# Two scaled chunks per output block, squares ahead of the last casts, and modulation dealt 5/5/2 over the thirds of a feed-forward stage

## The reference

```python
def modulate(x, g, shift, scale):
    return rmsnorm(x, g) * (1.0 + scale[:, None, :]) + shift[:, None, :]

def swiglu(h, w_gu, w_down):
    gu = h @ w_gu
    g, u = jnp.split(gu, 2, axis=-1)
    return (jax.nn.silu(g) * u) @ w_down

for l in range(DEPTH):                                  # DEPTH = 2
    mod = (c_act @ w_mod[l] + b_mod[l]).reshape(c.shape[0], N_MOD, D_MODEL)
    h = modulate(x, g_norm[l, 0], mod[:, 0], mod[:, 1])
    x = x + 0.5 * mod[:, 2][:, None, :] * swiglu(h, w_ffn1_gu[l], w_ffn1_down[l])
    h = modulate(x, g_norm[l, 1], mod[:, 3], mod[:, 4])
    x = x + mod[:, 5][:, None, :] * hybrid_mixer(h, ...)
    h = modulate(x, g_norm[l, 2], mod[:, 6], mod[:, 7])
    x = x + 0.5 * mod[:, 8][:, None, :] * swiglu(h, w_ffn2_gu[l], w_ffn2_down[l])
```

## Time and profile before

| | |
|---|---|
| runs (us) | 2893.82, 2894.48, 2900.41 |
| profiled execution (us) | 2897.52 |
| its span (us) | 2895.7 |
| mean granted TensorE clock | 0.978 |
| busy: PE, DVE, ACT, POOL | 96%, 47%, 37%, 39% |
| weights and modulation read | 368.23 MB, 130 GB/s |

### The profile page before, as it was taken

One profiled execution on the slowest core, in us unless ns is written; L12 is line 12 of the kernel. 1 busy time (PEld: TensorE's weight loads), 2 busy tenths in 40 slices (PEclk: granted clock), 3 DMA queues, 4 the chain that ended last, 5 costly groups with the idle time before them and its releaser, 6 DMA issues.

```text
span 2895.7 us, 34805 instructions
## 1 busy us (share of the span) xinstructions
PE 2777.8 (96%) x12952; PEld 2261.3 (78%) x12952; DVE 1360.8 (47%) x2214; ACT 1067.7 (37%) x1561; POOL 1140.2 (39%) x488
## 2 busy tenths in 40 slices
PE   6999999999999999999999999998989999999997
PEld 4888877778888788887777888887767778788886
DVE  5323257652324623237755242434654556673645
ACT  3222246442223422225543232354444453442322
POOL 2444443244444444444224444462211324344443
PEclk9999999999999999999999999998999999999998
DMA  7535442144445453443225353542200214222221
GB/s 284 204 117 188 155 151 88 58 161 176 159 145 187 169 182 138 174 168 124 73 73 189 139 207 132 204 164 81 73 30 15 73 61 151 102 102 102 97 92 44
DMA packets 70435, 378.82 MB, mean 131 GB/s; under 512 B 7904, under 2 KB 8672, under 8 KB 39808
## 3 DMA queue, kind: packets, MB, share of 16 engines
q1 hardware_dynamic: 65280, 358.56, 34.6%
q10 hardware_dynamic: 4992, 18.09, 1.7%
HBM read 368.23 MB, written 8.39 MB: 130 GB/s over the span
## 4 chain that ended last, share of the span: by engine, by line
PE 74%; DVE 12%; ACT 4%; issue 3%; DVEq 2%; ACTq 1%; DMA 1%; POOL 1%; SPq 1%; POOLq 0%
PE psum L514 20%; PE psum L516 20%; PE psum L515 20%; DVE psum L2152 2%; PE psum L977 2%; PE psum L999 1%; PE psum L533 1%; PE psum L535 1%; PE psum L534 1%; ACT w_hi L1092 1%; PE psum L664 1%; PE psum L665 1%; PE psum L987 1%; PE psum L666 1%; DVE psum L1655 1%
## 5 line engine op out<-in xcount | busy, mean ns | idle before, releaser
L437 POOL TENSOR_TENSOR w_lo<-raw,w_hi 128x1024 fp32r<-128x1024 f32 x464 | 1119.1, 2419 | 1566.4 <-ACT w_hi L1092 1556.3
L514 PE MATMUL psum<-h_hi,w_hi 128*128 128x512 f32 x1984 | 780.2, 393 | 14.4 <-DVE h_lo L1652 11.7
L1092 ACT CAST w_hi<-raw 128x1024 fp32r<-128x1024 f32 x464 | 480.9, 1047 | 810.0 <-PE psum L516 670.6
L515 PE MATMUL psum<-h_lo,w_hi 128*128 128x512 f32 x1984 | 775.5, 391 | 0.0
L516 PE MATMUL psum<-h_hi,w_lo 128*128 128x512 f32 x1984 | 775.5, 391 | 0.0
L514 PEld LDWEIGHTS psum<-h_hi,w_hi 128*128 128x128 f32 x1984 | 374.8, 189 | 101.2 <-DVE h_lo L1652 11.7
L516 PEld LDWEIGHTS psum<-h_hi,w_lo 128*128 128x128 f32 x1984 | 374.5, 189 | 79.1
L515 PEld LDWEIGHTS psum<-h_lo,w_hi 128*128 128x128 f32 x1984 | 374.9, 189 | 77.6 <-issue 0.5
L514 PE MATMUL psum<-hid_hi,w_hi 128*128 128x512 f32 x880 | 343.5, 390 | 5.9 <-DVE hid_lo L2158 5.9
L515 PE MATMUL psum<-hid_lo,w_hi 128*128 128x512 f32 x880 | 342.8, 390 | 0.0
L516 PE MATMUL psum<-hid_hi,w_lo 128*128 128x512 f32 x880 | 342.8, 390 | 0.0
(11 more groups left out here) (380 smaller groups left out, 3229.3 us busy)
## 6 DMA issues: line engine op xcount, KB each, us to landing
raw<-in_weights_dram SPq DMA_DIRECT2D x232, 1024.0 KB, 5.0
mod_raw<-in_mod_w_dram SPq DMA_DIRECT2D x192, 512.0 KB, 4.0
first_mods_a<-in_mod_w_dram SPq DMA_DIRECT2D x8, 512.0 KB, 11.2
first_mods_b<-in_mod_w_dram SPq DMA_DIRECT2D x8, 512.0 KB, 15.8
prod<-in_cond_rows_dram ACTq DMA_DIRECT2D x8, 512.0 KB, 3.4
first_mods_a<-gate_spill ACTq DMA_DIRECT2D x4, 1024.0 KB, 10.4
gate_spill<-gate_out_c ACTq DMA_DIRECT2D x5, 512.0 KB, 3.0
x<-in_xT_dram SPq DMA_DIRECT2D x1, 2048.0 KB, 8.5
```

The lines of the kernel that those rows point to most:

```text
L437: pool.tensor_tensor(w_lo[:, k % 2, cs], raw[:, k % 4, cs], w_hi[:, k % 2, cs].bitcast(F32), ALU.subtract).then_inc(lo_ready, 1)
L514: pe.matmul(out, wh, rhs_hi[:, c, :], start=(c == ks[0]), stop=False)
L515: pe.matmul(out, wh, rhs_lo[:, c, :], start=False, stop=False)
L1092: act.copy(w_hi[:, k % 2, cs], raw[:, k % 4, cs]).then_inc(hi_ready, 1)
```

## The change

It has five parts, all at the boundaries.

1. Scaled chunks: two per output block (0 and 1 after block 0, 2 and 3 after block 1, 4 and 5 after block 2), and 6 and 7 in the last block. For this DVE computes `a_col` earlier (`ahead_factors`, after the last up block of the last third, or after output block 0), and subtracts 0 and 1, 2 and 3, then 4, then 5 between the update of chunk 6 and its square (`last_quarter`).
2. In the last output block ACT squares chunk 6, scales it, squares chunk 7, scales it, and only then casts the second block's weights. Before, the casts stood ahead of the scaled chunks 5 to 7 (feed-forward) or ahead of both squares (mixers).
3. The bias sum is made in two parts, chunks 0 to 3 and 4 to 7, in two output blocks.
4. PE takes the column sums after the first half of chunk 2 (3 matmuls sooner) and spreads the norm after chunk 3 (6 matmuls sooner). `scale_first` becomes `scale_part`: the first bank after chunk 5 as before, the second after all 8 chunks. ACT's first SiLU waits for the first part, the copies of a mixer's and of the convolution's first block for both.
5. A third takes 5, 5 and 2 modulation positions instead of 4, 4 and 4.

```diff
+THIRD_MODS = (5, 5, 2)
-AHEAD_CHUNKS = ((), (0, 1), (2, 3, 4), (5, 6, 7))
+BIAS_PARTS = (range(0, 4), range(4, 8))
@@ PE, ahead @@
                         mm = pe.matmul(out, wl, xa_hi[:, c, :], start=False, stop=(c == KC - 1))
+                        if (c, t) == (2, 0):
+                            x_cols(r, n, i)
                     if c == KC // 2 - 1:
                         mm.then_inc(front_done, 1)
+                        rms_rows(r)
...
-                    if c == 2:
-                        x_cols(r, n, i)
-                    if c == 4:
-                        rms_rows(r)
@@ ACT @@
+            def last_chunks(i, n, xa_hi=h_hi):
+                for t in range(2):
+                    squares(n, 3, (t,))
+                    ahead(i, (6 + t,), xa_hi)
@@ ACT, first_taken (SiLU of the first block) @@
-                    act.wait_ge(scaled, first[0] + 1)
+                    act.wait_ge(scaled, 2 * first[0] + 1)
@@ ACT, ffn @@
-                        if j < 8 and j % 2 == 0 and mod in ROW_STARTS:
+                        if j < 2 * npos and j % 2 == 0 and mod in ROW_STARTS:
...
-                        if last and following is not None and j > count:
-                            ahead(following, AHEAD_CHUNKS[j - count])
+                            if following is not None:
+                                ahead(following, (2 * (j - count), 2 * (j - count) + 1))
@@ ACT, copies (mixer) @@
-                    act.wait_ge(scaled, first[0] + 1)
+                    act.wait_ge(scaled, 2 * first[0] + 2)
@@ ACT, mixer (the token mixer likewise) @@
                 for j in range(4):
+                    if j == 3:
+                        last_chunks(3 * l + 1, n + 1)
                     split_hi(g, k0 + MIX_IN_BLOCKS + j + 2, whole=(j < 2))
-                    squares(n + 1, j)
-                    if j:
-                        ahead(3 * l + 1, AHEAD_CHUNKS[j])
+                    if j < 3:
+                        squares(n + 1, j)
+                        ahead(3 * l + 1, (2 * j, 2 * j + 1))
@@ DVE @@
-            def prepare(q, following, early=0):
+            def ahead_factors(following):
                 i, g, k, at_shift, at_scale, gain, xa = following
-                if q == 1:
-                    factors(at_shift, at_scale, gain)
-                    dve.drain().then_inc(a_ready, 1)
-                if q == early:
-                    bias_sum(g, k, at_shift)
-                scaled_x(i, AHEAD_CHUNKS[q], xa)
+                factors(at_shift, at_scale, gain)
+                dve.drain().then_inc(a_ready, 1)
+
+            def prepare(q, following, early):
+                i, g, k, at_shift, at_scale, gain, xa = following
+                if early <= q < early + 2:
+                    bias_sum(g, k, at_shift, BIAS_PARTS[q - early])
+                scaled_x(i, (0, 1) if q == 0 else (2, 3) if q == 1 else (4,), xa)
+
+            def last_quarter(g, k, n, at, following):
+                i, xa = following[0], following[6]
                 dve.drain()
+                dve.wait_ge(half_done, at)
+                dve.scalar_tensor_tensor(x[:, 6, :], ...).then_inc(x_ready, 1)
+                scaled_x(i, (5,), xa)
+                add_squares(n, 3)
                 dve.wait_ge(block_done, 4 * g + k + 3)
+                dve.scalar_tensor_tensor(x[:, 7, :], ...).then_inc(x_ready, 1)
+                dve.drain().then_inc(out_free[k % 2], 1)
+                scaled_x(i, (6, 7), xa)
+
+            def scale_part(i, g, k, t):
+                if t == 0:
+                    dve.tensor_copy(ssq[:, :], psum[:, S_BANK + 1, :])
+                    dve.drain()
+                    dve.wait_ge(block_done, 4 * g + k + 3)
+                ps = psum[:, 2 * (k % 2) + t, :]
+                dve.tensor_tensor(ps, ps, ssq[:, :], ALU.mult)
                 dve.drain().then_inc(scaled, 1)
@@ DVE, norm @@
                     if first is not None and c == 5:
-                        scale_first(*first)
+                        scale_part(*first, 0)
                     dve.drain()
                 lo(DC - 1)
+                if first is not None:
+                    scale_part(*first, 1)
@@ DVE, mixer (early = 1; the token mixer and the feed-forward stages take early = 0) @@
+                for j in range(3):
                     add_to_x(g, k0 + MIX_IN_BLOCKS + j, j, n + 1)
+                    if j == 0:
+                        ahead_factors(following)
                     prepare(j, following, 1)
+                last_quarter(g, k0 + MIX_IN_BLOCKS + 3, n + 1, n + 1, following)
```

More of the change, by code:

```diff
@@ L1092, in split_hi, with squares @@
                     act.copy(w_hi[:, k % 2, cs], raw[:, k % 4, cs]).then_inc(hi_ready, 1)
-            def squares(n, q):
+            def squares(n, q, ts=(0, 1)):
                 act.wait_ge(sq_used, 4 * n + q + 1)
-                for t in range(2):
+                for t in ts:
                     act.wait_ge(x_ready, 8 * n + 2 * q + t + 1)
```

99 lines of the change are left out of this document (56 added, 43 removed).

## The result

The changed kernel takes 2870.84 us, the median of six runs (2870.06 to 2882.36); beside it the kernel before took 2895.03 (six runs, 2893.82 to 2900.41). The ratio is 0.9927 with a 95% interval of 0.9912 to 0.9941: 21 us faster by the ratio, 24 by the medians. The forecast was 2871, with 0.87 on faster. The profiled execution took 2870.46 us, its span is 2868.4 where it was 2895.7, and the mean granted clock 0.982 where it was 0.978.

What follows compares the result with a forecast made beforehand. PE's sequence was taken to bound the kernel (busy 96%), losing 50.9 us in twelve boundary blocks; 20.0 + 6.7 - 3.5 = 23.2 us saved gives 2871 us, range from just below 2864 to 2884.

Steps and rivals of the forecast that it cites:

- first blocks: First output block at each of six boundaries: 14.28 us each, 105.65 in sum before, 20.0 us saved.
- second blocks: Second output block at six boundaries: earlier spreading starts the norm earlier, PE's wait for normed differences nearly goes, 6.7 us saved.
- given back: Later second half of scaling delays POOL's weights in mixers (1.2 us each) and the convolution's fourth block (1.1): 3.5 us lost.
- the 15 that I had named as wrong: Sign against the forecast: any first block at a boundary taking above 15 us.
- chunks 0 to 5 earlier: Boundaries: earlier scaled chunks, with squares and chunks 6 and 7 ahead of casts, remove PE's first-block waits: 20.0 us saved.
- Modulation 5/5/2: Feed-forward thirds: pieces move to output blocks where DVE has slack; costed at nothing, up to 1 us a third lost.
- bank chain: Third blocks of feed-forward stages: PE waits for banks DVE frees after its last difference, 1.4 us twice and about 1.0.
- Bias and factors early: Boundaries: same instructions, costed at nothing with 1.6 us of cover at mixers' ends; one DVE holding by POOL costs nothing.
- A: Rival: chains behind the norm are shorter, all six third blocks start at 25.2 us; 30.5 us saved, 2864; 10%.
- B: Rival: in first blocks the clock stays low or the power is late; half the gain, 2885; 13%.
- C: Rival: mixers' DVE and ACT chains end at the same times and PE waits there; 2887 to 2890; 7%.
- D: Rival: ACT's casts come late behind scaled chunks, PE waits for weights in 18 output blocks; 2904; 4%.

## Why the prediction was right, and where it was not

*The total.* Right: 2871 forecast, 2870.84 measured (2868.73 when it ran again). The terms, in the trace: first blocks 20.0 forecast, 17.9 found; second blocks 6.7, found 6.0; given back 3.5, found 5.5; sum 23.2, found 18.5 at the boundaries and 8.8 elsewhere. So it is partly luck: three terms were each too good, by 4.7 us in all, and two gains that I had not seen made it up.

*First blocks.* 14.28 forecast, 14.10 measured in four. The other two reached 15.68, above the 15 that I had named as wrong, with PEclk 0.89. PE waits for nothing in them; I had argued from the sixth boundary of before, which kept the full clock, that small matmuls do no harm.

*Which part earns it.* This step failed. The prediction has "chunks 0 to 5 earlier" for the 20.0 us and "Modulation 5/5/2 ... Nothing". The runs say the reverse: 5/5/2 alone takes 15.8 us off the first blocks, chunks in their old places cost nothing, and the last casts first cost a few us at most. I had read the queue ahead of the late difference one step back, to ACT's casts, and not to why ACT was late with all of it: its 4.63 us of idle time for the factors, behind modulation pieces on DVE. I had looked at where the pieces went and found slack there; what mattered is where they had been. The two parts belong together in the code, since the pieces read the two banks that the scaled chunks are written to, so chunks 0 and 1 can stand in output block 0 only with the pieces gone from blocks 0 and 1. The changed kernel with 4/4/4 was not tried for that reason; with chunks and factors in their old places it could have run, and what the rest of the change is worth beside 4/4/4 is not measured.

*The final norm of layer 1.* No term. It is the same four pieces: they held ACT's split of the context, DVE's difference behind it, and the update of x6.

*Second blocks.* Right in mechanism and size: with the old places of sums and spreading the second blocks go back to 77.6, and PE waits for the differences again. Waits for banks at the third block were 0.8 to 0.9 us, for 1.4 and 1.0 forecast. That the bank chain "has the second half of the scaling in it either way" was wrong: scaled whole behind chunk 5, these waits vanish.

*Given back.* Mixers: 1.14 and 1.22 us of waiting for POOL, forecast 1.2 each, at 31.8 us after PE's start, forecast 32.0. Convolution: 1.1 and a wait of 2.01 us, where I had 1.1 in all, and then eight matmuls 0.43 us apart: the mechanism was right and the size off by the clock that fell behind the wait. Undoing this term gave 3.9 us by the medians and 3.6 by the blocks.

*Bias and factors early.* Nothing forecast, nothing found: the mixers' ends have no wait for weights. DVE's 8-element copy of the shift was held at five of the six boundaries, 1.16 us at three and 1.97 and 1.96 at the mixers' ends:

```profile
560.08 1.97 DVE L1606 COPY shift<-mods 128x8 f32<-128x8 f32 x1 [0.17 <-issue]
561.96 0.16 DVE L1607 TENSOR_SCALAR a_col<-mods 128x8 f32<-128x8 f32 x1
```

It ends with POOL's instruction each time (562.05 beside 562.02, 1469.92 beside 1469.90). One of the three is held, never the two behind it, and it is hidden, as I took it.

*The gain beyond 5/5/2.* By the trace the rest of the change shortens the twelve blocks by another 10.4 us, yet the two kernels' times agree within their intervals. 2.7 us of it is given back in the mixers and 2.7 in the convolution, 1.9 come in the token mixer, and most of the rest went to the clock: 122 matmuls of 512 columns at 1.2 GHz, against 90 and 93 in the two kernels with only the modulation moved, some 6 us. Why the changed kernel falls to the low clock more often is not settled; that it does in both of its profiles (122 and 125) is shown.

*Rivals.* A's figure (2864) was not reached by this kernel, nor quite by the one that is scaled whole in mixers and convolution (2867). B named the low clock in first blocks as a way to lose, and that is what took 3.2 us. C and D did not show.

## What to carry to other kernels

When an engine is late at the end of a chain, follow its queue back until it waited for nothing, and price what stood there; a part that moves work away must be priced where the work was, not only where it goes. Run the part that was costed at nothing first, by itself. An earlier consumer (the spreading) pays only when its producer is early too: undone in one kernel it cost 7.8 us in the second blocks, added alone to the other it brought none.

## What the runs showed of the hardware

PE falls to the low clock in a stretch in which it never waits. PE in the third first block after the change, behind the column sums:

```profile
951.65 1.03 PE L562 MATMUL psum<-ones,sq 128*128 128x1 f32 x8
952.54 0.49 PE L597 MATMUL psum<-h_hi,w_hi 128*128 128x512 f32 x1
...
953.57 0.51 PE L598 MATMUL psum<-h_lo,w_hi 128*128 128x512 f32 x1
...
954.30 0.63 PE L597 MATMUL psum<-h_hi,w_hi 128*128 128x512 f32 x1
954.73 0.63 PE L598 MATMUL psum<-h_lo,w_hi 128*128 128x512 f32 x1
```

From 953.9 on starts are 0.43 us apart where they were 0.23: 1.2 GHz, behind ten one-column matmuls that take 2.15 us (the profile shows each as two rows, so x8 is four). The spreading starts only at 955.58; in all 20 stretches counted below the clock fell before it, so the spreading's small matmuls are not what it fell behind. In the six profiles with ten in a row and next to no wait in the first block, 20 of 36 first blocks had such a stretch (changed kernel 2 and 3, sums late 1, last casts first 4, old chunks 6, scaled whole 4); with ten in two groups 1 of 6, with six 0 of 12. That fewer small matmuls in a row keep the clock up is what these counts suggest; no run shows the reason. A stretch costs 1.6 us. The Trainium skill (TensorE: Matmul & The Clock Gate, HAM oscillation — how this bites in real kernels) puts the fall down to idle gaps of PE. The kernel before fits that in part: in its first boundary's block the clock fell behind the wait of 2.03 us, but before that also behind column sums that had waited 1.32 us. These blocks, with PE busy 15.68 of 15.68 us, show the fall without a gap.

A one-column matmul of f32 with a 128x128 weight load costs 0.89 / 4 = 0.22 us of PE's time, as much as one of 512 columns of the split operands here (0.227).
